# Latent attention loop: where the high and low parts of a later head group are made

## The reference

```
def _attend_dense(q, k, v):
    s = jnp.einsum('bqhd,bkhd->bhqk', q, k, ...) * (QK_DIM ** -0.5)
    pr = jax.nn.softmax(s, axis=-1).astype(v.dtype)
    return jnp.einsum('bhqk,bkhd->bqhd', pr, v)
```

## Time and profile before

| | us |
|---|---|
| Median of 3 runs | 3233.27 |
| Lowest and highest | 3231.24 and 3234.66 |
| The profiled execution | 3228.83 |
| Its span, first to last instruction | 3226.9 |
| The loop, first exponentials to the last transposes | 2280.1 to 2588.9 |

### The profile page before, as it was taken

One profiled execution on the slowest core, in us unless ns is written; L12 is line 12 of the kernel. 1 busy time (PEld: TensorE's weight loads), 2 busy tenths in 40 slices (PEclk: granted clock), 3 DMA queues, 4 the chain that ended last, 5 costly groups with the idle time before them and its releaser, 6 DMA issues. The chain is left out here.

```text
span 3226.9 us, 40553 instructions
## 1 busy us (share of the span) xinstructions
PE 2822.9 (87%) x16494; PEld 2298.2 (71%) x16494; DVE 1547.7 (48%) x2189; ACT 1071.8 (33%) x1888; POOL 309.1 (10%) x308
## 2 busy tenths in 40 slices
PE   5999988999998988992987999988899988919997
PEld 4777777777678787881865888856677867817776
DVE  3225543443535214236535041025666654589997
ACT  4214311111215215232236112113555531207775
POOL 0004400000100000000000000002000010102333
PEclk9999999999999998995997889999999999959999
DMA  6554641121302111006523113121000045239997
GB/s 173 189 187 126 196 156 54 60 72 37 122 20 63 56 40 60 20 31 185 167 79 119 33 33 95 52 75 48 1 1 1 1 157 151 105 131 345 373 376 241
DMA packets 272228, 357.43 MB, mean 111 GB/s; under 512 B 54987, under 2 KB 185059, under 8 KB 270380
## 3 DMA queue, kind: packets, MB, share of 16 engines
q1 hardware_dynamic: 228332, 212.06, 20.5%
q0 software_dynamic: 32192, 121.81, 11.6%
q10 hardware_dynamic: 11520, 20.98, 1.8%
HBM read 282.70 MB, written 76.80 MB: 111 GB/s over the span
## 5 line engine op out<-in xcount | busy, mean ns | idle before, releaser
L225 PE MATMUL ps<-h_hi,st_w_lo 128*128 128x512 f32 x592 | 248.9, 420 | 15.3 <-PEq L834 9.5
L222 DVE TENSOR_TENSOR w_lo<-wraw,w_hi 128x1024 fp32r<-128x1024 f32 (+2 forms) x116 | 120.1, 1053 | 279.9 <-ACT w_hi L219 279.2
L222 DVE TENSOR_TENSOR ew_lo<-wraw,ew_hi 128x1024 fp32r<-128x1024 f32 x192 | 249.9, 1363 | 2.9 <-ACT ew_hi L219 2.6
L227 PE MATMUL ps<-h_hi,st_w_hi 128*128 128x512 f32 x592 | 234.4, 396 | 0.0
L226 PE MATMUL ps<-h_lo,st_w_hi 128*128 128x512 f32 x592 | 233.1, 394 | 0.0
L219 ACT ACTIVATE w_hi<-wraw 128x1024 fp32r<-128x1024 f32 (+2 forms) x116 | 104.1, 917 | 284.7 <-PE ps L227 148.0
L225 PE MATMUL ps<-w_hi,merged_lo 128*128 128x512 f32 (+2 forms) x408 | 160.1, 392 | 34.1 <-DVE w_lo L222 30.7
L219 ACT ACTIVATE ew_hi<-wraw 128x1024 fp32r<-128x1024 f32 x192 | 189.0, 1059 | 1.7 <-PE ps L227 1.7
L225 PE MATMUL ps<-h_hi,w_lo 128*128 128x512 f32 x384 | 156.7, 408 | 19.1 <-DVE w_lo L222 19.1
L225 PE MATMUL ps<-merged_hi,w_lo 128*128 128x512 f32 x400 | 160.4, 401 | 9.8 <-DVE w_lo L222 9.8
L226 PE MATMUL ps<-merged_lo,w_hi 128*128 128x512 f32 x400 | 159.8, 399 | 0.0
(11 more groups left out here) (499 smaller groups left out, 6500.2 us busy)
## 6 DMA issues: line engine op xcount, KB each, us to landing
wraw<-w_in SPq DMA_DIRECT2D x98, 512.0 KB, 4.9
wraw<-w_e_gate SPq DMA_DIRECT2D x64, 512.0 KB, 10.1
wraw<-w_e_up SPq DMA_DIRECT2D x64, 512.0 KB, 9.1
wraw<-w_e_down SPq DMA_DIRECT2D x64, 512.0 KB, 9.9
mod_w<-w_mod POOLq DMA_DIRECT2D x12, 2048.0 KB, 9.6
gates<-st_zo ACTq DMA_DIRECT2D x48, 256.0 KB, 2.0
rw_in<-rw_scan POOLq DMA_DIRECT2D x8, 1280.0 KB, 6.5
mg_gates<-gates POOLq DMA_DIRECT2D x16, 512.0 KB, 5.0
```

The lines of the kernel that those rows point to most:

```text
L222: return dve.tensor_tensor(dst, src, hi.bitcast(F32), ALU.subtract)
L225: pe.matmul(out, a[1], b[0], start=first, stop=False)
L227: return pe.matmul(out, a[0], b[0], start=False, stop=last)
```

## The change

A new tile `hs_` (named `mla_heads`) in SBUF holds two groups of fp32. For a later group ScalarE now runs two activations: it copies bank 7, times the gain, into `hs_` (counted by `ml_hev`), waits for that copy, and makes the high part from `hs_` (`high`, counted by `ml_hhi`). GpSimd subtracts the high part from `hs_` and writes the low part (counted by `ml_hsplit`). VectorE's L2590 is gone from the loop for the 30 later groups; the first ten groups are prepared as before. TensorE's waits on the low part at the transposes into bank 7 and at the next group become waits on ScalarE's copy; only the first scores of a head wait for GpSimd. The groups stand in the same iterations. The lines of the changed kernel are numbered a little higher than those of before: L2569 has become L2582 for a later group, L2601 L2622, L2605 L2626, L2606 L2627, L2628 L2649; the high part has the line of `high`, L219, and GpSimd's operation is L2603.

```
--- before
+++ after
@@
+                hs_ = sb(st, "mla_heads", [QKD, 2, 512])
...
                         if n >= 8:
-                            pe.wait_ge(S("ml_hlo"), n if n >= 10 else n - 7)
+                            pe.wait_ge(S("ml_hlo"), n - 7 if n < 10 else 10)
+                        if n > 10:
+                            pe.wait_ge(S("ml_hev"), n)
...
                             if t == 0:
-                                pe.wait_ge(S("ml_hlo"), 5 * h + 5 if h > 1 else 10)
+                                pe.wait_ge(*((S("ml_hsplit"), 5 * h - 5) if h > 1 else (S("ml_hlo"), 10)))
...
                         if n and next_head(n - 1):
                             hh, i = next_head(n - 1)
-                            pe.wait_ge(S("ml_hlo"), 5 * hh + i + 1)
+                            pe.wait_ge(S("ml_hev"), 5 * hh + i + 1)
...
+                    def later_head(h, i):
+                        _s, t0, w, dst = head_group(h, i)
+                        n = 5 * h + i
+                        act.wait_ge(S("ml_htr"), n + 1)
+                        if n >= 12:
+                            act.wait_ge(S("ml_hsplit"), n - 11)
+                        act.activation(hs_[:, n % 2, 0:w * P], ps[0:QKD, 7, 0:w * P], ACT.Copy,
+                                       scale=gcol[:, int(i >= 2):int(i >= 2) + 1]).then_inc(S("ml_hev"), 1)
+                        act.wait_ge(S("ml_hev"), n + 1)
+                        high(act, dst[0], hs_[:, n % 2, 0:w * P]).then_inc(S("ml_hhi"), 1)
...
                         if next_head(n):
-                            head(*next_head(n))
+                            later_head(*next_head(n))
+
+                @block.gpsimd
+                def _(gp):
+                    for n in range(10, 5 * HEADS):
+                        _s, t0, w, dst = head_group(*divmod(n, 5))
+                        gp.wait_ge(S("ml_hhi"), n - 9)
+                        gp.tensor_tensor(dst[1], hs_[:, n % 2, 0:w * P], dst[0].bitcast(F32), ALU.subtract
+                                         ).then_inc(S("ml_hsplit"), 1)
...
-                    def row_max(n, next_=None):
+                    def row_max(n):
...
-                            if i == 1 and next_:
-                                head(*next_)
...
-                            row_max(n + 2, next_head(n))
+                            row_max(n + 2)
```

## The result

| | before | after |
|---|---|---|
| Median, us | 3233.78 (7 runs) | 3210.57 (7 runs) |
| Lowest and highest | 3231.24 and 3237.84 | 3204.93 and 3223.45 |
| The profiled execution | 3228.83 | 3204.93 |
| Its span | 3226.9 | 3203.1 |
| In it, first exponentials to the last 512-column copy of probabilities | 308.14 | 291.83 |

The ratio of the times is 0.9939, with a 95% interval from 0.992 to 0.9958: 23 us faster, where 7.0 were forecast. The last two rows of the table take the profiled executions apart: of the 24.0 us between them the loop gave **16.3**, and 7.7 lie outside it, where no instruction has changed.

What follows compares the result with a forecast made beforehand. TensorE, busy 72.6 of 78 us, was taken as nearest to a bound, with holes to win. Gains of 5.9 + 0.9 + 0.2 = 7.0 us from the median 3233.27 gave 3226.3 us, range 3216 to 3238.

Steps and rivals of the forecast that it cites:

- Where the loop stands and what a subtraction costs: In the loop, one VectorE subtraction costs 0.67 us in an even iteration, delaying the exponentials; an odd one also costs 0.67.
- The early release of bank 7: TensorE's transposes behind nine odd groups wait for ScalarE's copy, not the low part: gain 9 x 0.65 = 5.9 us.
- rival (1): L2606 is not held by GpSimd, so 0.67 us returns in 15 places: 15.5 us gained, 3217.8 us; chance 0.27.
- ScalarE's addition costs nothing: ScalarE's second activation per group, 0.63 us, fits before its next copy with 0.13 us of cover, or slips harmlessly.
- Rival (3): ScalarE becomes the bound through a long hand-over to its own second activation: 3236.2 us; chance 0.09.
- a dead heat that VectorE wins: In even full-width places GpSimd's 1.29 us operation and L2605 start together, at 2456.88 and 2456.87; VectorE goes first.
- I take held: L2606, the row maximum's last step, waits for GpSimd's end, leaving 15 x 0.06 = 0.9 us; forecast case, chance 0.36.
- the prediction's two cases: L2606 held by GpSimd, 7.0 us gained, chance 0.36; or not held, 15.5 us gained, chance 0.27.
- Held until when: The held L2606 ends about 0.12 us after GpSimd's operation, at 2458.29.
- Half-width groups: In six even iterations L2605 is held 0.22 us, leaving 0.03 of 0.25 each: 6 x 0.03 = 0.2 us.
- Rival (2): GpSimd wins the dead heat and holds L2605, moving what follows 1.16 us from its free place: 3234.5 us; chance 0.28.
- The range: Median of the changed kernel between 3216 and 3238 us, taking in rivals (1) and (2).

Runs made afterwards that it cites:

- e4_bank_wait: Changed kernel with TensorE's transposes into bank 7 waiting for the high part instead of ScalarE's copy; loop 296.52 us against 291.83.
- e2_two_elements: Changed kernel with the last step of the row maximum (L2627) on two elements per partition instead of one; loop 300.17 us against 291.83.
- e8_after_max: Changed kernel with GpSimd's subtraction also waiting until that iteration's row maximum is done; loop 290.35 us against 291.83.
- e5_short_copy: Changed kernel with ScalarE's copy of bank 7 made without its scale, 0.59 instead of 0.68 us; loop 305.97 us against 291.83.
- e3_pool_early: Changed kernel with an added GpSimd subtraction of the group from itself as soon as it is copied, before the real one; loop 296.92 us against 291.83.

## Why the prediction was wrong, step by step

- **Where the loop stands and what a subtraction costs: right.** 0.67 us in an even iteration: pair 1 went from 10.02 to 9.35, and product to exponentials is 2.00 again. No group costs more than before except in pair 4.
- **The early release of bank 7, 9 x 0.65 = 5.9 us: right in kind, and about right in size.** The wait on the low part is gone from TensorE. e4_bank_wait, which puts 0.67 of the 0.78 us back, takes 4.7 us; the other 0.11 in nine places would make it 5.7, an estimate. The place behind an odd group gained more than that: pair 3 took 0.67 us more than pair 1 before and takes 0.12 less now, 0.79 in all. Against it the pairs that hold a full-width group in both iterations gained 0.53 instead of 0.67. Net that is the 0.65 of the forecast, but from two terms, of which its sum had one (rival (1) had the other, as 0.1 in six pairs). What the 0.79 holds beyond the wait on the bank was not tested.
- **ScalarE's addition costs nothing: right.** 631 ns each where 0.63 was taken. ScalarE's next copy in pair 2 waited 0.15 us for TensorE, the cover forecast as 0.13. Behind the odd group the copy (2367.37) follows the high part at once, with no wait for TensorE, so it has slipped as forecast, and pair 3 is the shorter for all that. Rival (3) is out.
- **GpSimd, 1.29 us for 512 columns, and a dead heat that VectorE wins: right.** It takes 1.27 to 1.28 alone, 1.31 to 1.32 where VectorE was let through. The meeting takes place 14 times and not 15 (not at the loop's first group). There L2626's record starts between 5 ns after and 3 ns before GpSimd's, and is never held.
- **"I take held", for the last step: this is the step that failed.** It had L2606 wait until GpSimd ends, and so left 15 x 0.06 = 0.9 us of what is 15 x 0.67, less a little in the pairs with two full groups (0.53 in pair 2). The last step ran beside GpSimd in 24 places and took its 0.27 us in all of them. The 128x16 copy of the earlier trace rows was the wrong neighbour: it shares the one SBUF input and the SBUF output, but not the one element per partition. Two elements are held and one is not (e2_two_elements), and that is worth 8.3 us of the loop; the prediction's two cases lay 15.5 - 7.0 = 8.5 apart. The right case was named, rival (1), priced at 15.5 us where the loop gave 16.3, and given 0.27.
- **Held until when: nearly right.** The held last step was to end 0.12 us behind GpSimd; in e2_two_elements it ends 0.03 behind, and the held maxima 0.01 to 0.02. That, 15 x 0.09, is more than the 1.0 by which the case came out above its forecast (8.0 and not 7.0).
- **Half-width groups, 0.03 left of 0.25 each: right in size.** L2626 takes 373 to 443 ns there, so it is held by 0.21 to 0.28 where 0.22 was forecast. The change loses in pair 4 by it (e8_after_max gives 0.30 back in the third quarter, 0.22 in the first two).
- **Rival (2): real, and 0.09 us away.** "It decides from GpSimd's start about 0.05 us before L2605's": with 0.09 it decides (e5_short_copy), with 0.00 it does not, and in e3_pool_early the maximum is held once with GpSimd 0.06 ahead (by 61 ns; 0.69 us). Its price, 1.16 us a place, was 1.05. A ScalarE copy that is 0.09 us shorter is all that separates this kernel from it. The kernel before had a place with a lead of 0.05 us already, ahead of the loop, where VectorE's operation takes 0.31 us; at 2255.81, with GpSimd 0.03 behind, the same one takes 0.17:

```profile
2263.60 0.32 POOL L2405 TENSOR_TENSOR fT<-mla_q,hn_qtab 128x64 f32<-128x64 f32 x1
2263.65 0.31 DVE L2378 TENSOR_SCALAR mla_rsq<-hn_ss 128x32 f32<-128x32 f32 x1
```

- **The range.** Even around the right case it would have missed the median. 3233.27 - 16.3 is 3217.0, and the first measurement gave 3210.57. The difference lies outside the loop, where executions of one kernel differ by some 10 us; the range took no account of that. The seven runs of the changed kernel alone spread over 18.5 us.

## What to carry to other kernels

Ahead of an operation on GpSimd, list what VectorE has with SBUF operands in the stretch it will cover, by kind of operation, number of inputs and elements per partition, and put GpSimd's start behind the last of those that somebody waits for: one wait did that here and took away a loss of 14 us that lay 0.09 us off. Most of the gain of "moving work to another engine" was here in two other things, the work's place in VectorE's order and the bank that comes free with the copy; moving it behind the row maximum on the same engine gives 13.2 of 16.3 us. Where whole executions wander by more than the change is worth, measure it as a stretch between two fixed rows of the profile, which here repeated within 0.15 us.

## What the hardware showed that was not expected

- A tensor_scalar of one element per partition, SBUF to SBUF with two per-partition scalars, is not held by GpSimd: 0.27 us in 64 of 64, 24 of them over a GpSimd operation. With two elements it took 0.80 us (even) and 1.14 (odd).
- Who is held is settled within less than a tenth of a us: with the two starts within 5 ns VectorE went through and GpSimd took some 0.03 us longer; with GpSimd 0.06 and 0.09 us ahead VectorE's two-input maximum was held, and with 0.05 us a tensor_scalar of 128x32.
- A GpSimd tensor_tensor of 96x512 took 1.28 us, and 1.04 with both inputs from the same tile.
- VectorE's RECIPROCAL of 128x2 in SBUF, over a GpSimd operation in 21 places of e8_after_max, kept its 0.15 to 0.16 us, where the tensor_scalar of 128x2 was held in all 24.
